# An nsa stage whose attention steps are bundled between half units of weights, with 512-column values and a compressed softmax in two halves

## What is computed

```python
q, k_c, v_c, k_s, v_s, k_w, v_w, gates = split(h @ w_in)       # 16 query heads in 4 groups, 4 heads each
gates = sigmoid(gates).reshape(B, S, 3, G, R)
def compress(kv, pos, w1, w2):                                 # 15 blocks of 32 tokens, stride 16
    blk = kv[:, cmp_idx] + pos
    return gelu(blk @ w1) @ w2
kc, vc = compress(k_c, ...), compress(v_c, ...)
p_cmp = masked_softmax(q @ kc, cmp_mask);  o_cmp = p_cmp @ vc
o_slc = attention(q, k_s, v_s)    # causal: 256 tokens are 4 blocks, and all are selected
o_win = attention(q, k_w, v_w)    # causal: the window of 512 is longer than the sequence
o = gates[0] * o_cmp + gates[1] * o_slc + gates[2] * o_win
return o @ w_out
```

## Time and profile before

| | us |
|---|---|
| median of 3 runs | 2257.91 |
| lowest and highest | 2255.97, 2258.14 |
| the profiled execution | 2253.36 |
| its span in the profile | 2251.2 |
| TensorE busy | 2202.5 |
| DVE busy | 1784.3 |
| ACT busy | 1164.8 |

### The profile page before, as it was taken

One profiled execution on the slowest core, in us unless ns is written; L12 is line 12 of the kernel. 1 busy time (PEld: TensorE's weight loads), 2 busy tenths in 40 slices (PEclk: granted clock), 3 DMA queues, 4 the chain that ended last, 5 costly groups with the idle time before them and its releaser, 6 DMA issues.

```text
span 2251.2 us, 37874 instructions
## 1 busy us (share of the span) xinstructions
PE 2202.5 (98%) x15228; PEld 1968.7 (87%) x15228; DVE 1784.3 (79%) x3504; ACT 1164.8 (52%) x2044; POOL 0.2 (0%) x4
## 2 busy tenths in 40 slices
PE   7999999999999999999999999999999999999998
PEld 7878889898889988896988887898888889989998
DVE  7788978689887898878898766577877876478888
ACT  4685556565543655448655634544222136376433
POOL 0000000000000000000000000000000000000000
PEclk9999999999999999999999999999999999999999
DMA  7416665466565666650666532024554523334563
GB/s 243 142 60 222 235 199 203 153 213 234 195 217 171 213 234 193 219 204 21 215 237 204 177 121 77 1 76 152 175 171 157 168 89 107 131 97 159 207 223 124
DMA packets 70158, 373.57 MB, mean 166 GB/s; under 512 B 7392, under 2 KB 16736, under 8 KB 37984
## 3 DMA queue, kind: packets, MB, share of 16 engines
q1 hardware_dynamic: 61472, 361.52, 47.2%
q10 hardware_dynamic: 8512, 9.63, 1.4%
HBM read 369.03 MB, written 1.05 MB: 164 GB/s over the span
## 4 chain that ended last, share of the span: by engine, by line
PE 86%; DVE 8%; ACT 3%; DMA 2%; issue 1%; ACTq 0%; DVEq 0%
PE ps L494 82%; DVE w_lo L2009 2%; DMA w_raw<-weights 2%; DVE hid_f L2392 1%; PE ps L838 1%; DVE hid_f L2414 1%; PE ps L775 1%; ACT w_hi L1345 1%; PE ps L822 1%; ACT hid_f L1545 0%; DVE X L2282 0%; PE ps L763 0%; DVE a_both L2009 0%; ACT p_ring L1483 0%; DVE X L2135 0%
## 5 line engine op out<-in xcount | busy, mean ns | idle before, releaser
L494 PE MATMUL ps<-a_both,w_hi 128*128 128x256 f32 (+1 forms) x4864 | 1057.5, 328 | 17.4 <-DVE a_both L2066 10.4
L494 PEld LDWEIGHTS ps<-a_both,w_hi 128*128 128x128 f32 x4864 | 808.3, 190 | 92.1 <-issue 15.3
L2009 DVE TENSOR_TENSOR w_lo<-w_raw,w_hi 128x1024 fp32r<-128x1024 f32 (+1 forms) x632 | 708.2, 1149 | 93.1 <-ACT w_hi L1345 84.5
L494 PE MATMUL ps<-a_both,w_lo 128*128 128x256 f32 (+1 forms) x3136 | 714.5, 292 | 0.0
L1345 ACT CAST w_hi<-w_raw 128x1024 fp32r<-128x1024 f32 (+2 forms) x446 | 412.7, 974 | 349.7 <-DMA w_raw<-weights 348.1
L494 PEld LDWEIGHTS ps<-a_both,w_lo 128*128 128x128 f32 x3136 | 521.2, 191 | 24.1
L494 PE MATMUL ps<-hid_both,w_hi 128*128 128x512 f32 (+2 forms) x2216 | 529.0, 348 | 5.4 <-DVE qk L3040 1.1
L494 PEld LDWEIGHTS ps<-hid_both,w_hi 128*128 128x128 f32 x2216 | 381.9, 189 | 59.6 <-issue 10.3
L494 PE MATMUL ps<-hid_both,w_lo 128*128 128x256 f32 (+2 forms) x1460 | 340.5, 305 | 0.0
L494 PEld LDWEIGHTS ps<-hid_both,w_lo 128*128 128x128 f32 x1460 | 236.5, 190 | 17.0
L1351 ACT CAST w_hi<-w_raw 128x1024 fp32r<-128x1024 f32 (+2 forms) x186 | 190.2, 1023 | 3.1 <-DMA w_raw<-weights 2.9
(11 more groups left out here) (236 smaller groups left out, 1906.6 us busy)
## 6 DMA issues: line engine op xcount, KB each, us to landing
w_raw<-weights SPq DMA_DIRECT2D x250, 1024.0 KB, 4.8
pe_sb<-weights SPq DMA_DIRECT2D x96, 512.0 KB, 5.6
w_raw<-weights SPq DMA_DIRECT2D x64, 704.0 KB, 4.0
pe_sb<-na_bias ACTq DMA_DIRECT2D x32, 128.0 KB, 2.2
X<-x_t SPq DMA_DIRECT2D x2, 512.0 KB, 6.9
X<-c_rows ACTq DMA_DIRECT2D x2, 512.0 KB, 4.2
qk<-qk ACTq DMA_DIRECT2D x4, 256.0 KB, 6.9
qk<-ctx_t ACTq DMA_DIRECT2D x1, 1024.0 KB, 5.5
```

Source lines behind the costliest of these rows:

```text
L494: return nc.tensor.matmul(out, stationary, moving, start=start, stop=stop)
L2009: return v.tensor_tensor(out, a, b.bitcast(F32), ALU.subtract)
```

## The change

- **Order of the units** in the nsa stage: keys and values to be compressed, gates (a unit of its own), queries 0, queries 1, selected keys, `compress(0, 0)`, window keys, `compress(0, 1)`, `compress(1, 0)`, `compress(1, 1)`, upper values, lower values (both branches at once, 512 columns), the small unit, queries 2, queries 3, four output units.
- **Attention steps** begin after the compression and stand between the two halves of units: step 1 inside the upper values, step 3 inside the lower values, step 6 inside queries 2, step 8 inside queries 3. Scores have one pair of banks, (6, 7). There are four slots for probabilities and for their transposes, where there were three.
- **The compressed branch** is done in two halves of 8 heads: scores, shift, exp, normalization, transposes. Its products are separate (`compressed`), added to a tile when its two steps are done.
- **Moved between engines:** the compressed values go from PSUM to their place on ACT, where DVE did this, and so do both values; the memsets cover only the padding.

The core of the diff ("..." where something is left out):

```diff
-    "nsa": [UC] * 13 + [SMALL_UNIT] + [UC] * 5,
+    "nsa": [UC] * 2 + [GATE_UNIT] + [UC] * 10 + [SMALL_UNIT] + [UC] * 6,
...
+            def upper_values(between):
+                u, _ = unit(cnt, "")
+                first = cnt.n["A"]
+                start_product("A", first)
+                value_half(u, 0, 0, first)
+                between()
+                start_product("A", first + 1)
+                value_half(u, 0, 1, first + 1).then_inc(unit_done, 1)
...
-                for kv in range(2):
-                    for h in range(2):
-                        compress(kv, h)
-                        if (kv, h) != (1, 1):
-                            fm_unit("AA", a)
-                values_unit()
...
+                compress(0, 0)
+                fm_unit("AA", a)
+                keys_formed = cnt.n["A"]
+                compress(0, 1)
+                compress(1, 0)
+                compress(1, 1)
...
+                pe.wait_ge(nsa[j]["gates"], j + 1)
+                scores(0)
+                upper_values(second_steps)          # scores(1), gelu_turns()
+                scores(2)
+                turn(0)
+                lower_values(fourth_steps)          # scores(3), turn(1)
+                scores(4)
+                turn(2)
+                compressed_keys_values()
+                scores(5)
+                turn(3)
+                pe.wait_ge(taken["D"], cnt.n["D"])
+                pe.wait_ge(taken["A"], cnt.n["A"])
+                values(0)
+                compressed_scores(0)
+                queries(seventh_steps)              # scores(6), turn(4), values(1)
+                compressed_turns(0)
+                scores(7)
+                turn(5)
+                values(2)
+                queries(ninth_steps)                # scores(8), turn(6), values(3), compressed(0), compressed(1)
+                scores(9)
+                turn(7)
+                values(4)
+                compressed_scores(1)
...
+                compressed(3)
+                values(8)
+                compressed_turns(1)
+                scores(12)
...
+                out((0, 1, 2))
+                turn(15)
+                values(14)
+                out((3, 4))
+                values(15)
+                compressed(7)
+                out((5, 6, 7))
```

The same on ACT, from the first exps to the first half of the compressed softmax:

```diff
+                gelu(1, v_unit)
+                exps(0)
+                ahead(v_unit)
+                skip("")
+                exps(1)
+                copy(0)
+                exps(2)
+                u, made = next_unit("AA")
+                value(0, made[0])
+                copy(1)
+                exps(3)
+                value(1, made[1])
+                ahead(u)
+                copy(2)
...
+                exps(4)
+                wait(act, v_ready, v_count)
...
+                for r in range(REP):
+                    rows = slice(32 * r, 32 * r + 32)
+                    ins = nc.scalar.copy(v_blk[rows, :, r, :], ps[rows, v_bank, 0:KV].rearrange("p (g d) -> p g d", g=GROUPS))
+                ins.then_inc(taken["D"], 1)
+                copy(3)
+                exps(5)
+                compressed_exp(0)
```

And on DVE, the front of the stage and the stretch around the second half of the softmax:

```diff
                 unit_around(compressed(1), lambda u: first_positions(0))
+                skip("A")
+                dve.wait_ge(taken["A"], cnt.n["A"])
                 unit_around(queries(0), lambda u: first_positions(1))
                 unit_around(queries(1), lambda u: moved_positions(0))
                 blocks_low(0)
-                unit_around(queries(2), lambda u: moved_positions(1))
+                unit_around(lambda pair: k_sb[:, pair, 0:S], lambda u: moved_positions(1))
                 skip("")
-                ahead(scaled_unit(queries(3)))
-                step(v.memset(vg_hi.bitcast(F32), 0.0))
+                ahead(keys(1))
+                padded = p_cmp.rearrange("p (n c) -> p n c", c=32)[:, :, CS:32]
+                step(v.memset(padded, 0.0))
                 skip("")
                 blocks_low(1)
...
+                ahead(u)
+                reduce(9)
+                normalize(8)
+                compressed_shift(1)
+                reduce(10)
+                normalize(9)
+                compressed_p(1)
+                cnt.next("A")
+                reduce(11)
+                normalize(10)
+                low(2)
+                reduce(12)
+                normalize(11)
+                low(3)
+                split_half(q_unit + 2, 0)
```

More of the change, by code:

```diff
@@ new lines, in turn, with values, compressed @@
+                def turn(i):
+                    pe.wait_ge(m["p_ready"], i + 1)
+                    wait(pe, m["t_taken"], i)
+                    pair_turn(name, i, STEP_T)
+                def values(i):
+                    pair_values(name, i, STEP_O)
+                def compressed(t):
+                    pair, r = divmod(t, REP)
+                    pe.wait_ge(nsa[j]["cmp_t_taken"], pair + 1)
+                    for e in range(2):
+                        g = 2 * pair + e
+                        last = nc.tensor.matmul(ps[half(e), STEP_O[t % 2], 0:S], v_sb[:, 3, (g * REP + r) * HD:(g * REP + r + 1) * HD],
+                                                v_sb[:, 2, g * S:(g + 1) * S], start=False, stop=True, skip_group_check=True)
+                    last.then_inc(nsa[j]["cmp_done"], 1)
@@ new lines, in run_nsa @@
+                queries(seventh_steps)
[8 more added lines that the diff above has]
+                compressed_scores(1)
+                scores(10)
+                turn(8)
+                values(5)
+                compressed(2)
+                values(6)
+                scores(11)
+                turn(9)
@@ new lines, in run_nsa @@
+                compressed_exp(0)
+                ahead(small_unit)
+                copy(4)
+                exps(6)
+                skip("AA")
+                compressed_copy(0)
+                copy(5)
+                exps(7)
+                copy(6)
+                exps(8)
+                high(0)
+                high(1)
+                skip("AA")
+                copy(7)
+                exps(9)
+                compressed_exp(1)
+                copy(8)
+                exps(10)
+                high(2)
@@ L1675, in run_nsa @@
+                copy(9)
+                exps(11)
+                high(3)
+                compressed_copy(1)
+                copy(10)
+                exps(12)
+                copy(11)
+                exps(13)
+                high(4)
+                copy(12)
+                exps(14)
+                high(5)
+                copy(13)
+                exps(15)
+                copy(14)
+                high(6)
+                copy(15)
+                high(7)
                 if j == 0:
@@ new lines, in run_nsa @@
+                dve.wait_ge(s["gates"], j + 1)
+                normalize(0)
+                ahead(v_unit)
+                reduce(2)
+                normalize(1)
+                skip("")
+                gelu_parts()
+                reduce(3)
+                normalize(2)
+                u, _ = next_unit("AA")
+                reduce(4)
+                normalize(3)
+                split_half(u + 2, 0)
+                small_unit, _ = unit(cnt, "DD", STEP_O)
+                reduce(5)
+                normalize(4)
@@ new lines, in run_nsa @@
+                split_half(u + 2, 1)
+                compressed_shift(0)
+                u, evict = query_unit(2)
+                evict(0)
+                reduce(6)
+                normalize(5)
+                compressed_p(0)
+                evict(1)
+                ahead(small_unit)
+                cnt.next("A")
+                reduce(7)
+                normalize(6)
+                reduce(8)
+                normalize(7)
+                q_unit, evict = query_unit(3)
+                evict(0)
```

517 lines of the change are left out of this document (285 added, 232 removed).

## The result

| | before | after |
|---|---|---|
| median | 2257.31 (2255.97 to 2258.14, 4 runs) | 2293.31 (2292.05 to 2295.82, 4 runs) |
| span of the profiled execution | 2251.2 | 2291.2 |
| mean granted clock of the profiled execution (1 is 2.4 GHz) | 0.995 | 0.986 |
| TensorE's named waits in the second stage | 7.3 | 19.1 |

The change makes the kernel slower: ratio 1.0163, interval 1.0151 to 1.0176. That is 36 us, 18 per nsa stage, where 9.4 had been forecast; between the two profiled executions it is 40 us. It lies above the forecast's range of 2255 to 2290. The direction was right.

The account below looks back on a forecast made before the run. TensorE, busy 2202.5 of 2251.2 us, was taken as the bound. Per stage 4.35 + 3.8 plus 1.3 for the clock made 9.4, 18.8 for two, so a median of 2276.7 us, range 2255 to 2290.

Parts of the forecast that it names:

- The wait for hid_both: Ahead of compress(1, 0): TensorE waits 6.98 us instead of 1.07, as the low half stands behind a split awaiting a load.
- The front: Start of the stage: 2.75 us of moved gate work plus 1.6 of new waiting, so compress(1, 0) starts 4.35 us later.
- The two waits in the steps: Attention steps: TensorE waits 2.4 us for ACT's copies ahead of values(0) and 2.7 for low(2) ahead of values(8).
- The clock: Granted clock per stage: 1.3 us lost after the long wait, 3.3 at the compressed scores no longer lost.
- The restart behind the long wait: TensorE after the wait of 7 us: slow clock costs 1.3 us per stage, bounds 0 and 3.3.
- the walk: Engine programs followed in written order from compress(1, 0) to the stage's end: 107.6 us against 103.8, 3.8 longer.
- The loss of 3.3 that I took as saved: Compressed scores: about 6.6 us at half clock now, a loss of 3.3 per stage, counted as gone with the change.
- The Trainium skill's rule: TensorE's clock: an idle array falls back to throttled; a cold restart in each stage, without which the sum is 2.6 us smaller.
- Steps fill perfectly: Rival, attention steps: DVE never idle after the first scores, end 10.5 us earlier, -2.4 per stage, total 2253; chance 0.08.
- half of it: Rival, attention steps: DVE idles 5 us, 2.9 per stage with no cold restart, 2263 to 2264; chance 0.17.
- The change doesn't cut the step waits: Rival, attention steps: DVE and ACT stay the bound, 5.9 us more waits, 15.3 per stage, 2288; chance 0.06.
- A second fall of the clock: Rival, small unit to compressed scores: 3.3 us more per stage, up to 2 more at the long wait, 2283 to 2287; chance 0.17.

Follow-up runs that it names:

- e1: The changed kernel with blocks_low(1) in DVE's program put ahead of the split of the unit after next; 2277.4 us, ratio 1.0091.
- e5: e4 with the split due after the gate unit put behind the block positions in DVE's program; 2267.08 us, ratio 1.0055.
- e2: The changed kernel with 28 unused matmuls of 512 columns issued on TensorE while it waits for blocks_ready; 2288.67 us, ratio 1.0145.
- e4: e1 with low(2) put ahead of reduce(11) and normalize(10) in DVE's program; 2266.35 us, ratio 1.0052.
- b3: The kernel before with blocks_low(1) ahead of the split and 8 unused 512-column matmuls between the 32-column compressed scores; 2256.19 us, ratio 1.0011.
- e7: e5 with ACT's four copies of the compressed values put ahead of exps(4) instead of behind it; 2257.08 us, ratio 1.0015.
- e3: The changed kernel with 14 unused 512-column matmuls in the small unit and ahead of the wait for the compressed values; 2286.2 us, ratio 1.0139.
- c1: The kernel before with only the change's new order of units around the block compression; 2268.74 us, ratio 1.0065.

## Why the prediction was right and wrong

- **The wait for hid_both: right.** Forecast 6.98, measured 6.93 and, by the order alone, 6.6. That DVE's written order puts it there is shown by e1, which takes 5.0 us of it away.
- **The front: mechanism right, size short.** I had 1.6 us of new waiting and `compress(1, 0)` 4.35 late; it is 5.8 late. The term that was short is DVE's wait of about 3 us for the split ahead of the first drain. It is 4.98. The second unit ends where the gates begin, at 968.41, and the cast of what is loaded in its place comes at 975.20:

```profile
968.41 0.40 PE L488 MATMUL ps<-a_both,w_hi 128*48 128x256 f32 x2
...
975.20 2.00 ACT L1459 CAST w_hi<-w_raw 128x1024 fp32r<-128x1024 f32 x2 [3.48 <-DMA w_raw<-weights]
...
976.28 2.36 DVE L2187 TENSOR_TENSOR w_lo<-w_raw,w_hi 128x1024 fp32r<-128x1024 f32 x2 [4.98 <-ACT w_hi L1459]
```

  That is 6.8 us from a unit's end to the cast, where I took the 5.0 of another place, and the 1.8 between them are nearly all that the wait is longer. Here the load shares the queues with the shifts of the block's inputs (`qk<-qk`, issued by ACT at 969.07). That those are the cause is argued, not shown.
- **The two waits in the steps: right.** On ACT's copies 2.4 forecast, 1.49 measured (2.1 in e1 and in e5's second stage, where the clock is higher ahead of it); a copy takes 0.37, forecast 0.38. On low(2) 2.7 forecast, 2.52 measured.
- **The clock: the step that failed.** Of the sum's 9.4 per stage, 1.3 were for the clock behind the long wait, and the 3.3 lost before were taken as saved; by the stretches the clock costs 10.4. Three parts. The restart behind the long wait was priced from the start of the program; e2 puts it at 2.0 to 2.8. The second fall stood among the rivals with 0.17 and 3.3 us; it came, and lasts 13.7 us in place of some 6.8 of before, so it costs 6.1. A third fall, behind the wait for low(2), I had not thought of: in e4, without that wait, it is gone. The extra 9 us are the gap between the 5 forecast and the 13.6 measured for the rest of the stage; the waits in that part were not short in the walk, 11.6 us against 8.4 that the trace names.
- **The loss of 3.3 that I took as saved** was the error in reasoning: nothing I had read showed that halving the compressed scores keeps the clock up, and the clock was down through the first half of them all the same. I counted the clock as a property of the narrow stretch, and wrote down waits of 2.4 and 2.7 us without asking what each does to it.
- **The Trainium skill's rule** (TensorE: Matmul & The Clock Gate, "The HAM clock gate"), that an idle array falls back to the throttled state: the trace agrees at the long wait, where 6.93 us without a matmul are followed by half speed, and e2, with the same wait filled, stays at 1.00. Other rows the rule doesn't explain, and they decide: in b3 and in the kernel before the clock falls while TensorE is busy 5.00 of 5.00 us, and the fall at 1040 comes ahead of the wait.
- **The rivals.** *Steps fill perfectly* and *half of it* left no trace: the waits for hid_f fell by 1.3 us only. *The change doesn't cut the step waits*, which had a chance of 0.06, came nearer than I thought: with the new waits for the reduce they are 4.4 us for 4.8. *A second fall of the clock* came true, with 6.1 us where I had 3.3, and a third with it.

**What stays open:** what decides whether the clock falls, and for how long. Taking a pause of 2.1 us away raised it in most executions (e7 against e5); in the kernel after and in e5's first stage the fall began ahead of the pause, with the same narrow work that in e7's trace does no harm; in b3 wide matmuls between the narrow ones helped in some executions and not in the median, in e3 they did with the pause filled too.

## What to carry to other kernels

Read an engine's program for what is written behind a wait on a load: an instruction whose inputs are long there, as the low half here, goes ahead of it, since the unit of work that hides the order today may be moved away tomorrow. Price a new wait of TensorE with what the clock does around it: here taking away waits of 2.1 to 2.5 us gave 4 to 5 per stage. Where the clock is in play, look at the mean clock of several executions before you read one trace. And before a bundling is judged, mend these waits: the same design was 1.6% slower as it stood and 0.15% slower with four instructions moved, which is still no gain.

## What was not expected of the hardware

- A wait of 2.14 us is followed by half speed up to about 1031.6 in e5's second stage, and one of 0.35 us at the same place by none in e7's trace.
- A fall lasted about 6.8 us before and 13.7 us in the kernel after.
- The same program takes its falls at different places and lengths: e1's trace has one behind the front wait of the second stage (0.66 from 970 to 975), the kernel after none; b3's ten executions range over mean clocks of 0.992 to 0.997.
- The clock falls while TensorE is busy without a gap, also with matmuls of 512 columns among those of 32 (b3).
- The kernel of c1 holds the clock at 1.00 through steps in which TensorE is busy 3.73 of 5.00 us (1045 to 1050): the gaps there are many and short.

```profile
1045.00:1050.00 5.00, 3.73 (x50) 2.47 (x52) 4.47 (x27) 5.00 (x19) 0.00 (x0) 1.00 0.01 3
```
